# An attention core worked by pairs of heads, on one Trainium2 core

## The reference

```python
q = apply_rope(rms_norm(q, q_gain), cos, sin) * (HEAD_DIM ** -0.5)   # 16 heads of 64
k = apply_rope(rms_norm(k, k_gain), cos, sin)                        # 4 heads of 64, one for 4 query heads
s = jnp.einsum('bqhgd,bkhd->bhgqk', qb, k).astype(jnp.float32)
p = jax.nn.softmax(s, axis=-1).astype(v.dtype)
return jnp.einsum('bhgqk,bkhd->bqhgd', p, v)
...
return o @ w_o
```

## Time and profile before

| what | value |
|---|---|
| median of 3 runs | 1137.19 us (1136.44 to 1138.9) |
| the profiled execution: span from its first to its last instruction | 1134.5 us |
| what lies around the span (median less span) | 2.7 us |
| TensorE busy | 1094.0 us, 96% |
| VectorE busy / ScalarE busy | 717.5 us, 63% / 556.7 us, 49% |
| attention core, first transposes to the output projection | 290.1 to 352.9 us |
| busy there: TensorE / ScalarE / VectorE | 61.85 / 34.37 / 31.99 us of 62.8 |

### The profile page before, as it was taken

One profiled execution on the slowest core, in us unless ns is written; L12 is line 12 of the kernel. 1 busy time (PEld: TensorE's weight loads), 2 busy tenths in 40 slices (PEclk: granted clock), 3 DMA queues, 4 the chain that ended last, 5 costly groups with the idle time before them and its releaser, 6 DMA issues.

```text
span 1134.5 us, 21273 instructions
## 1 busy us (share of the span) xinstructions
PE 1094.0 (96%) x8622; PEld 1048.0 (92%) x8622; DVE 717.5 (63%) x1036; ACT 556.7 (49%) x830; POOL 114.5 (10%) x103
## 2 busy tenths in 40 slices
PE   6999999999999999999999999999997699999998
PEld 5999999998547999999999999999997699999997
DVE  5766655575554666665467666544889967666542
ACT  4544454453556554444445454444596556454541
POOL 3000000043000200000010000000377401000000
PEclk9999999999999999999999999999998899999999
DMA  8654445715002254635653644457153163645541
GB/s 250 212 190 148 162 149 184 247 61 174 1 1 73 77 186 158 203 111 182 198 187 127 201 155 148 150 184 243 55 186 111 38 223 112 211 160 176 170 137 38
DMA packets 166464, 169.65 MB, mean 150 GB/s; under 512 B 3312, under 2 KB 165416, under 8 KB 166392
## 3 DMA queue, kind: packets, MB, share of 16 engines
q1 hardware_dynamic: 166088, 168.16, 45.5%
q0 software_dynamic: 96, 0.28, 0.1%
q10 hardware_dynamic: 208, 0.20, 0.1%
HBM read 167.30 MB, written 1.05 MB: 148 GB/s over the span
## 4 chain that ended last, share of the span: by engine, by line
PE 88%; DVE 8%; ACT 1%; issue 1%; DMA 1%; POOL 0%; SPq 0%; DVEq 0%; ACTq 0%
PE bank L358 25%; PE bank L360 25%; PE bank L359 25%; PE bank L607 2%; PE bank L579 2%; DVE h L1120 1%; PE bank L593 1%; PE bank L386 1%; DVE mg L1116 1%; DVE xl L1083 1%; PE bank L366 1%; DVE gm L1368 1%; PE bank L479 1%; PE bank L377 1%; PE bank L374 1%
## 5 line engine op out<-in xcount | busy, mean ns | idle before, releaser
L1077 DVE TENSOR_TENSOR wl<-raw,wh 128x2048 fp32r<-128x2048 f32 (+2 forms) x178 | 366.3, 2078 | 173.8 <-ACT wh L717 173.4
L358 PE MATMUL bank<-xh,wl 128*128 128x272 f32 (+1 forms) x1552 | 448.5, 289 | 9.3 <-DVE xl L1373 7.8
L360 PE MATMUL bank<-xh,wh 128*128 128x272 f32 (+1 forms) x1552 | 446.6, 288 | 0.0
L359 PE MATMUL bank<-xl,wh 128*128 128x272 f32 (+1 forms) x1552 | 445.1, 287 | 0.0
L717 ACT ACTIVATE wh<-raw 128x2048 fp32r<-128x2048 f32 (+2 forms) x177 | 299.4, 1714 | 97.6 <-PE bank L360 97.6
L358 PEld LDWEIGHTS bank<-xh,wl 128*128 128x128 f32 x1552 | 293.5, 189 | 10.8 <-DVE xl L1373 8.0
L360 PEld LDWEIGHTS bank<-xh,wh 128*128 128x128 f32 x1552 | 293.4, 189 | 0.0
L359 PEld LDWEIGHTS bank<-xl,wh 128*128 128x128 f32 x1552 | 293.4, 189 | 0.0
L358 PE MATMUL bank<-ah,wl 128*128 128x272 f32 (+1 forms) x704 | 201.5, 286 | 0.0
L360 PE MATMUL bank<-ah,wh 128*128 128x272 f32 (+1 forms) x704 | 201.1, 286 | 0.0
L359 PE MATMUL bank<-al,wh 128*128 128x272 f32 (+1 forms) x704 | 201.0, 286 | 0.0
(11 more groups left out here) (157 smaller groups left out, 1181.2 us busy)
## 6 DMA issues: line engine op xcount, KB each, us to landing
raw<-in_ffn_w_in SPq DMA_DIRECT2D x88, 1024.0 KB, 5.3
raw<-in_ffn_w_out SPq DMA_DIRECT2D x32, 768.0 KB, 5.1
raw<-in_ffn_w_out SPq DMA_DIRECT2D x32, 640.0 KB, 4.2
raw<-in_rec_w_in SPq DMA_DIRECT2D x8, 1024.0 KB, 5.4
raw<-in_attn_w_qkv SPq DMA_DIRECT2D x6, 1024.0 KB, 5.0
raw<-in_attn_w_o SPq DMA_DIRECT2D x4, 1024.0 KB, 5.4
raw<-in_rec_gate_w SPq DMA_DIRECT2D x16, 256.0 KB, 3.7
raw<-in_rec_w_out SPq DMA_DIRECT2D x4, 1024.0 KB, 5.2
```

The lines of the kernel that those rows point to most:

```text
L358: pe.matmul(dst, b, mh, start=first, stop=False)
L359: pe.matmul(dst, a, ml, start=False, stop=False)
L360: return pe.matmul(dst, a, mh, start=False, stop=last)
L1077: dve.tensor_tensor(wl[:, slot(u), 0:kn * 256], w, wh[:, slot(u), 0:kn * 256].bitcast(F32), ALU.subtract).then_inc(w_ready, 1)
```

## The change

The core goes by steps instead of tiles: for each kv head one step with the tile of the last tokens, and four steps with a pair of heads and one half of the tokens each, 20 steps in all. In a step of a pair:

- the two score products go to two banks of one tensor (`SCORE[s % 2]`), one from partitions 0 to 63 and one from 64 to 127, one behind the other;
- one `tensor_reduce` takes both maxima (544 elements), and one reciprocal makes both factors; the exponentials and the multiplications stay one per head;
- six transposes go to two of three banks (`flipped`), chosen by a table (`TURN`) so that the step shares one bank with the step before it, and one `place` copies both (768 elements in a row of 96 partitions);
- `weigh` takes both heads for half of the tokens (128 or 144 columns), alternating between output partitions 0 to 63 and 64 to 127.

The output's high part is now VectorE's too (`out_split`), and there is one output bank. The small jobs of the Q projection stand inside the products, behind k = 4, and one tile nearer to their input; the first scores are inside the last product. Three pieces of group 0 of the output projection (`begin_wo`, now in banks 6 and 7) stand in the last steps, and only k = 7 is left behind. The two `keep_warm(4, ...)` and `spread_r(1)` with its wait are gone; the wait that VectorE has for it in the next feed-forward counts one less.

```diff
-        S_BANK = (bank[0], bank[1], bank[6], bank[7])
+        QSUM, ROTB, QSCALE = bank[5], bank[3], bank[4]
+        SCORE = (score_even, score_odd)
...
+                def scores(s):
+                    j, q = divmod(s, STEPS_S)
+                    if s >= 2:
+                        pe.wait_ge(p_exp, first_tile(s - 1))
+                    dst = SCORE[s % 2]
...
+                        for e in range(2):
+                            o = HD * e
+                            last = pe.matmul(dst[:, e, 0:L], qt[o:o + HD, 2 * j + i, P * half:P * half + P],
+                                             kd[o:o + HD, j, :], start=True, stop=True)
+                    last.then_inc(s_done, 1)
+
+                def turn(s):
+                    for i, (e, b, placed) in enumerate(TURN[s]):
+                        if placed:
+                            pe.wait_ge(pt_ready, placed)
+                        pe.wait_ge(p_norm, first_tile(s) + i + 1)
+                        for c, k0 in enumerate(KTOK):
+                            last = pe.transpose(flipped[0:KT, b, P * c:P * c + P], prow[:, 2 * (s % 2) + e, k0:k0 + KT], ident)
+                        last.then_inc(t_done, 1)
+
+                def weigh(s):
+                    j, i, half = pair_of(s)
+                    pe.wait_ge(pt_ready, s + 1)
+                    if half == 0 and 2 * j + i:
+                        pe.wait_ge(o_ready, 2 * j + i)
+                    cols = slice(P, L) if half else slice(0, P)
+                    for c in range(3):
+                        for e in range(2):
+                            last = pe.matmul(weighed[HD * e:HD * e + HD, cols], vt[:, c, HD * j:HD * j + HD],
+                                             pt[:, j % 2, c, 2 * i + e, cols], start=c == 0, stop=c == 2, skip_group_check=True)
+                    if half:
+                        last.then_inc(pv_done, 1)
...
                     for k in range(KC):
                         last = product(bank[t % 2][:, 0:L], U_QKV + 2 + (t - KT_N) // 2, 2 * k + t % 2,
                                       xh[:, k, :], xl[:, k, :], k == 0, k == KC - 1)
-                        if t == KT_N and k == 3:
-                            spread_r(1)
+                        if t == KT_N and k == 2:
+                            pe.wait_ge(v_ready, 3)
+                            head_means(0)
+                            rotate(0)
+                        if k == 4:
+                            head_means(t - 1)
+                            rotate(t - 1)
+                            if t > KT_N:
+                                spread_scale(t - 2)
+                        if t == QKT - 1 and k == 4:
+                            pe.wait_ge(k_dup, 32)
+                            scores(0)
...
+                for s in range(STEPS):
+                    if s + 2 < STEPS:
+                        scores(s + 2)
+                    if s == 0:
+                        pe.wait_ge(q_final, QKT)
+                    if s >= STEPS - 2:
+                        begin_wo(3 * (s - STEPS + 2), 3 * (s - STEPS + 2) + 3)
+                    turn(s)
+                    if s >= 1 and (s - 1) % STEPS_S:
+                        weigh(s - 1)
+                begin_wo(6, 7)
+                weigh(STEPS - 1)
...
+                for s in range(STEPS):
+                    normalise(s)
+                    if s >= 2 and (s - 2) % STEPS_S:
+                        j, i, half = pair_of(s - 2)
+                        if half:
+                            out_split(2 * j + i)
+                    if s + 2 < STEPS:
+                        maximum(s + 2)
```

More of the change, by code:

```diff
@@ L89, with first_tile, turning, pair_of @@
 NPROJ = 6
-TILES_S = 9
+STEPS_S = 5
+STEPS = NKV * STEPS_S
+def first_tile(step):
+    j, q = divmod(step, STEPS_S)
+    return 9 * j + max(0, 2 * q - 1)
+def turning():
+    plan, last = [], {0: 0, 1: 0, 2: 0}
+    for s in range(STEPS):
+        j, q = divmod(s, STEPS_S)
+        if q == 0:
+            used = [(0, min(last, key=lambda b: last[b]))]
+        else:
+            banks = ((0, 1), (1, 2))[q % 2]
+            used = sorted(enumerate(banks), key=lambda eb: last[eb[1]])
+        plan.append([(e, b, last[b]) for e, b in used])
+        for e, b in used:
+            last[b] = s + 1
+    return plan
+TURN = turning()
+def pair_of(step):
+    j, q = divmod(step, STEPS_S)
+    i, half = divmod(q - 1, 2)
+    return j, i, half
 def shape_constants():
@@ L251, in build @@
         ACC = 8
[L253 to L260, removed]
         def ffn_banks(m):
@@ L583, in turned @@
[L583 to L610, removed]
+                        spread_scale(0)
@@ L625, in attention @@
-                tiles = NKV * TILES_S
-                scores(2)
-                for a in range(tiles):
-                    if a + 3 < tiles:
-                        scores(a + 3)
-                    turn(a)
-                    j, t = divmod(a - 1, TILES_S)
-                    if a >= 1 and t >= 2 and t % 2 == 0:
-                        weigh(j, (t - 2) // 2)
-                weigh(NKV - 1, GROUP - 1)
+                for s in range(STEPS):
[8 more added lines that the diff above has]
+                        weigh(s - 1)
@@ L902, in out_high @@
-                def out_high(pair):
-                    act.wait_ge(pv_done, pair + 1)
-                    act.activation(xh[:, pair, :], bank[4 + pair % 2][:, 0:L], ACT.Copy).then_inc(oh_ready, 1)
-                tiles = NKV * TILES_S
-                exponent(0)
-                exponent(1)
-                for a in range(tiles):
-                    if a + 2 < tiles:
-                        exponent(a + 2)
-                    place(a)
-                    j, t = divmod(a - 2, TILES_S)
-                    if a >= 2 and t in (4, 8):
-                        out_high(2 * j + (t == 8))
@@ L917, in attention @@
+                exponents(0)
+                for s in range(STEPS):
+                    if s + 1 < STEPS:
+                        exponents(s + 1)
+                    place(s)
                 high(U_WO + 3, 0)
```

154 lines of the change are left out of this document (76 added, 78 removed).

## The result

The changed kernel takes 1122.72 us (median of 4 runs, 1121.95 to 1124.99) against 1136.96 for the kernel before: a ratio of 0.9877, 95% interval 0.9864 to 0.9889. It is faster, by 14.2 us; 1115.0 was forecast, and the range ended at 1121. The core did what the prediction said. 9 us of its gain were given back in the Q projection in front of it.

What follows compares the result with a forecast made beforehand. TensorE was taken to bound the kernel. Core saving 22.8 us less 0.6 in the Q projection gave 22.2, taking the span from 1134.5 to 1112.3; with 2.7 up to the median, the forecast was 1115.0 us, range 1111 to 1121.

Steps and rivals of the forecast that it cites:

- What bounds the core, and the price of a pair: Core: TensorE bounds it and pairs cost what one costs; gains 10.4 us scores, 10.4 `weigh`, 1.9 transposes.
- The two rows that decided it: Old trace: neighbouring score products took 0.73 us against 0.72 for one; spreads over both column halves 0.65 against 0.64.
- the estimate of 1119.7: Core pairs at 79% of ideal: 0.12 us more per score pair, 0.17 per `weigh`, 4.7 us in all.
- The other engines follow: Core steps: ScalarE needs 1.66 us and VectorE 1.79 where TensorE takes 2.32; 0.4 us of waits over 20 steps.
- The ends of the core: TensorE idles 1.4 us at the core's front and 1.1 us behind the last `weigh`.
- The Q projection: Before the core: dropping `spread_r(1)` saves 0.64 us, first two tiles wait 0.7 and 0.6; the stage ends 0.6 later.
- The clock: Rival, in the core: waits lower TensorE's clock to 1.2 GHz, 32 us of streamed work doubles, 1147 us; chance 0.04.
- The fourth rival: Core as fast as told, but end waits grow or small jobs stall every tile (8 x 0.6): 1119 to 1120; chance 0.08.
- the sum: From 281.3 to 352.9: 48.8 us instead of 71.6, saving 22.8; less 0.6 in the Q projection, 22.2 us.
- The 2.7 us that the forecast put on top: Whole kernel: the profiled span lies 2.7 us below the median of runs, so span 1112.3 became forecast 1115.0.

Runs made afterwards that it cites:

- the kernel with the lows later: The changed kernel with VectorE's low halves of the output projection's second and third weight units moved one tile on: 1114.15 us, ratio 0.9809.
- the kernel with the scores apart: The changed kernel with those low halves one tile on and the odd head's score product between the two heads' transposes: 1130.6 us, ratio 0.9944.
- the old core: The kernel before with only the Q projection's small jobs moved inside the product from its second tile, ScalarE's roots one tile earlier: 1146.91 us, ratio 1.0088.

## Why the prediction was wrong

- **What bounds the core, and the price of a pair.** Right. 0.65 predicted and 0.66 measured for scores, 0.83 and 0.91 against 0.81 and 0.89 for `weigh`, 0.80 against 0.79 for transposes, 0.81 against 0.806 for a placing, 0.74 against 0.72 for a maximum. The two rows that decided it were accidents of the old order: two neighbouring scores at 288.97, and the spreads. (16 x 0.80 + 4 x 0.46 is 14.6 and not 14.7; that changes nothing.) The 79% of the Trainium skill for column tiles (TensorE: Matmul & The Clock Gate, Measured speedup vs the span model), and the estimate of 1119.7 from it, are not borne out by these rows.
- **The other engines follow.** Right: ScalarE idles 12.9 us before placings, and within the core the chain shows waits of about 0.1 us only (before 313.44), three times.
- **The ends of the core.** Right: 1.11 us behind the last `weigh` (1.1 predicted). At its head TensorE waited 0.49 + 0.24 + 0.51 = 1.24 us where 1.4 were predicted, and in the first two Q tiles 0.62 and 0.77 where 0.7 and 0.6 were.
- **The Q projection.** This is the step that failed: "Later tiles have 4.2 us between the same two points", and behind it "The DMA queue, weights and `low`s keep their places in order". I counted the `low` behind tiles 2 to 4, whose high half is made beforehand, and took its 2.29 us for the price in every tile. Behind tiles 5 and 7 the `low` waits for a `high` of 1.91 us that ScalarE starts after the tile's copy. From the end of tile 5's product to the factor of tile 4 that is about 5.4 us (265.9 to 271.3). TensorE asks for this factor in tile 6. Now that is five of eight k (1.9) and two jobs (1.0) behind the product of tile 5, about 3 us (TensorE's wait begins at 268.96). Before, it was three jobs, the whole product of tile 6 and two jobs, 5.9 us in the trace (261.9 to 267.87): just enough. The order of VectorE's queue had not changed; the point where TensorE asks had.
- **The clock.** The rival was the right mechanism at another place: not the packed core (1.00 there in the kernel with the lows later) but the two gaps of 2.4 us in front of it. With the products without use in them the clock stayed full. Its own place was not safe either: with one more wait of 1.28 us at the core's head the clock fell there too, in the kernel with the scores apart.

The fourth rival named the failed step, "the small jobs stall in every tile because VectorE's factor is late", at 4.8 us with 0.08; it was 4.8 us in two tiles, and nothing was added for the clock behind a gap. With that step mended the kernel takes 1114.15 us; from the means of h on, its trace has 48.0 + 45.2 - 5.25 + 1.1 = 89.1 us where the kernel before has 111.3, 22.2 less, the amount of the sum. Its span in the trace is 1112.3 us, the one predicted. The 2.7 us that the forecast put on top were too much: every run lies 1.7 to 1.9 us above its own span, and the rest of the 2.7 is the difference between the profiled execution and the median.

## What to carry to other kernels

When a consumer is moved forward, walk the producer's queue for each iteration apart, and write behind every instruction in front of the product what that one waits for: the stall here came from a wait of the neighbour in the queue. A gap on TensorE can have two prices, its length and the slow stretch behind it. The two of 2.40 us had both here, a lone one of 1.1 us only the first. Count both, and give the gap work if it can't be closed. In this kernel small products paired for nothing where they used opposite halves of the array and stood next to each other in the queue, alternating; look in the old trace for places where they already do. And compare traces over the part that was changed: the rest differed by up to 2.4 us between executions.

## What the hardware showed that was not expected

- After an idle gap of 2.40 us the granted clock was 0.50 for 4.7 us and 0.85 in the 5 us behind; after the second, as long, it was 0.63 over 3 us and 0.88 over the next 5: two equal gaps, and stretches at 0.50 of about 6.8 and 3.4 us by these rows. The same two falls came with the old core (0.85 and 0.93 in the same stretches). In the profiled run of the changed kernel a gap of 1.11 us (before 346.75) was not followed by one. In the kernel with the scores apart waits of 0.49, 0.24, 0.52 and 1.28 us within 8 us were, with a clock of 0.50 for 10 us.
- A lone score product costs 0.65 us, a pair side by side 0.66, and a pair in two places 1.30.
- Twelve instructions that alternate between column halves take 0.81 us, the same twelve sorted by half 1.07, with the second half's row starting 0.28 us late: the order of issue counts also where there is no wait between them.
